# A two-block transformer step in fp32 on one core: negated maxima as a row of the queries, rotary halves added by transfers, input blocks and taps moved

## The reference

```python
u_l, cq_l, ckv_l, kr_l = mixer_inputs(x * (1 + sc1) + sh1, w_in[i])
k_nope_l, k_rope_l, v_l = mla_keys_values(ckv_l, kr_l, kv_norm_g[i], w_ukv[i], cos, sin)
q_nope_l, q_rope_l = mla_queries(cq_l, q_norm_g[i], w_uq[i], cos, sin)
attn_l = attend_blocked(...)          # softmax over 256 context and 512 own keys, 8 heads
conv_l = conformer_conv(u_l, conv_dw_w[i], conv_dw_b[i], conv_ln_g[i], conv_ln_b[i])
y_l = merge_groups(conv_l, attn_l, w_o[i], b_o[i])
x_mid = layer_norm(ALPHA * x + g1 * y_l, ln1_g[i], ln1_b[i])
f_l = conv_ffn(x_mid * (1 + sc2) + sh2, ...)

def attend(q_nope, q_rope, k_nope, k_rope, v):
    s = (q_nope . k_nope + q_rope . k_rope) * SOFTMAX_SCALE      # 64 and 32 wide
    return softmax(s) . v

def apply_rope(x, cos, sin):
    return jnp.concatenate([x1 * cos - x2 * sin, x2 * cos + x1 * sin], axis=-1)

def conformer_conv(u, dw_w, dw_b, ln_g, ln_b):       # u is 2 x 512 channels
    a, gte = jnp.split(u, 2, axis=-1)
    v = dwconv(a * jax.nn.sigmoid(gte), dw_w, dw_b)  # 31 taps, each channel for itself
    return jax.nn.silu(layer_norm(v, ln_g, ln_b))
```

## Time and profile before

| What | Value |
|---|---|
| median of 3 runs | 1101.9 us (1100.87 to 1102.03) |
| the profiled execution | 1101.06 us |
| its span, first to last instruction | 1099.2 us |
| TensorE busy | 98% |
| VectorE, ScalarE, GpSimd busy | 70%, 51%, 11% |
| mean granted clock of TensorE | 0.999 |
| weight stream and other HBM reads | 132.45 MB |

### The profile page before, as it was taken

How to read it: one execution, slowest core, us unless ns; L and a number is a source line. 1 busy time by engine, 2 the same in 40 slices (tenths; PEclk the granted TensorE clock), 3 DMA queues, 4 the chain that set the end, 5 groups by cost and what they waited for, 6 DMA issues and landing times.

```text
span 1099.2 us, 16381 instructions
## 1 busy us (share of the span) xinstructions
PE 1072.9 (98%) x6595; PEld 889.3 (81%) x6595; DVE 773.7 (70%) x1259; ACT 563.9 (51%) x1022; POOL 120.6 (11%) x152
## 2 busy tenths in 40 slices
PE   7989999999999999999999999999999999999997
PEld 4778888888888788888878777888888888888886
DVE  6978889878677747658886788777665656545427
ACT  6576566656333447764366775575444444431211
POOL 0222121112322000100211113000000000000001
PEclk9999999999999999999999999999999999999999
DMA  9743433346355753131342553222222323252202
GB/s 379 295 184 116 154 135 126 126 172 202 103 199 216 285 213 125 42 127 47 77 95 52 127 127 86 77 77 86 107 99 93 108 84 116 77 210 78 84 31 77
DMA packets 26550, 143.23 MB, mean 130 GB/s; under 512 B 3009, under 2 KB 3433, under 8 KB 12650
## 3 DMA queue, kind: packets, MB, share of 16 engines
q1 hardware_dynamic: 19936, 128.46, 32.6%
q0 software_dynamic: 4176, 7.60, 4.0%
q10 hardware_dynamic: 2362, 6.12, 1.6%
HBM read 132.45 MB, written 2.12 MB: 122 GB/s over the span
## 4 chain that ended last, share of the span: by engine, by line
PE 78%; DVE 10%; ACT 6%; issue 2%; DMA 2%; POOL 1%; DVEq 0%; SPq 0%; ACTq 0%; POOLq 0%
PE PB L185 76%; ACT WH L199 2%; DVE WL L206 2%; PE PB L193 2%; DVE RAW L1515 1%; DVE CV L214 1%; DMA RAW<-in_wstream 1%; POOL UPA L206 1%; DMA XL<-in_x 1%; DVE PX L237 1%; ACT XL L200 0%; DMA CV<-DG 0%; ACT L200 0%; ACT PTA L200 0%; DVE XL L214 0%
## 5 line engine op out<-in xcount | busy, mean ns | idle before, releaser
L185 PE MATMUL PB<-HH,WH 128*128 128x512 f32 (+1 forms) x880 | 338.4, 385 | 4.3 <-DVE HL L206 2.0
L185 PE MATMUL PB<-HH,WL 128*128 128x512 f32 (+1 forms) x880 | 333.0, 378 | 0.0
L206 DVE TENSOR_TENSOR WL<-RAW,WH 128x1024 fp32r<-128x1024 f32 (+3 forms) x172 | 196.5, 1149 | 192.3 <-ACT WH L199 191.9
L185 PE MATMUL PB<-HL,WH 128*128 128x512 f32 (+1 forms) x880 | 331.0, 378 | 0.0
L199 ACT ACTIVATE WH<-RAW 128x1024 fp32r<-128x1024 f32 (+3 forms) x172 | 166.8, 976 | 267.9 <-PE PB L185 231.7
L185 PEld LDWEIGHTS PB<-HH,WH 128*128 128x128 f32 x880 | 165.6, 188 | 36.8 <-issue 1.8
L185 PEld LDWEIGHTS PB<-HH,WL 128*128 128x128 f32 x880 | 165.6, 188 | 31.5 <-issue 0.2
L185 PEld LDWEIGHTS PB<-HL,WH 128*128 128x128 f32 x880 | 165.8, 188 | 29.7 <-issue 0.2
L185 PE MATMUL PB<-WL,AH 128*128 128x512 f32 (+1 forms) x198 | 72.5, 366 | 0.0
L185 PE MATMUL PB<-WH,AH 128*128 128x512 f32 (+1 forms) x198 | 72.5, 366 | 0.0
L185 PE MATMUL PB<-WH,AL 128*128 128x512 f32 (+1 forms) x198 | 72.4, 366 | 0.0
(11 more groups left out here) (308 smaller groups left out, 1748.2 us busy)
## 6 DMA issues: line engine op xcount, KB each, us to landing
RAW<-in_wstream SPq DMA_DIRECT2D x101, 1024.0 KB, 4.9
EARLY<-in_wstream SPq DMA_DIRECT2D x7, 1024.0 KB, 13.8
RAW<-in_wstream SPq DMA_DIRECT2D x5, 768.0 KB, 4.4
CV<-DG POOLq DMA_DIRECT2D x15, 256.0 KB, 3.3
TMP<-TMP POOLq DMA_DIRECT2D x14, 256.0 KB, 3.3
RAW<-in_wstream SPq DMA_DIRECT2D x5, 512.0 KB, 3.7
XL<-in_x SPq DMA_DIRECT2D x2, 1024.0 KB, 6.7
HB<-in_x SPq DMA_DIRECT2D x2, 1024.0 KB, 5.9
```

Source lines behind the costliest of these rows:

```text
L185: return self.put(lambda e: e.matmul(o, l, r, start=start, stop=stop, skip_group_check=skip))
L206: return self.put(lambda e: e.tensor_tensor(o, a, b, op))
```

## The change

1. **Maxima as a row.** `KR[96:128]` is no longer a copy: row 96 is one, the others zero. ScalarE copies only rows 0 to 95 of a query and writes into rows 96 to 127 the broadcast row of negated maxima, which TensorE makes once a head with the matrix of ones and `DGR` (`query_row`); the low part has zeros there (`no_rest`). A score tile then is three matmuls. In tile 0 of heads 0, 2, 4, 6 and 7 (`late`) the old form stays, over 96 rows, and the row is made behind it; for heads 1, 3 and 5 it is made between the two parts of the keys. There is one `DGR` instead of two.
2. **Rotary parts.** As the rows 96 to 127 no longer count, the two products are added explicitly: for heads 0 and 1 by VectorE (through `QS`), for the others by an accumulating transfer of 32 rows (`add_turned`), for which `query_high` waits; it moves from tile 4 to tile 5.
3. **Last input blocks.** `u2(3)` stands in the stream and on TensorE behind query 0, keys 0 and query 1, as blocks 88 and 89 instead of 84 and 85. The high parts of queries 0 and 1 overwrite two of its operand's tiles, hence the marks `("last", 0)` and `("last", 1)`.
4. **Taps.** The last six taps of tiles 0 and 2 are products on ScalarE and transfers (`more_product`, `add_more`) in tiles 1 and 5 of heads 0 to 5, so VectorE has 81 tap instructions. The square of tile 0 moves to tile 4 of head 3. The sums of the convolution tiles go from GpSimd to VectorE (`norm_sums`).

```diff
-QUERY_BLOCK, KEY_BLOCK, VALUE_BLOCK = (86, 89, 90, 92, 93, 96, 97, 99), (87, 91, 95, 98), (88, 94)
+QUERY_BLOCK, KEY_BLOCK, VALUE_BLOCK = (84, 86, 90, 92, 93, 96, 97, 99), (85, 91, 95, 98), (87, 94)
...
+    def late(h):
+        return h not in (1, 3, 5)
...
-    CONV_AT = {"75a": 2, "75b": 4, "76": 3, "78": 3, "79": 3, "81": 2, "82": 2, "83": 6, "84": 6, "85": 6, "86": 2, "86b": 2}
+    CONV_AT = {"75a": 2, "75b": 4, "76": 3, "78": 3, "79": 3, "81": 2, "82": 2, "83": 6, "84": 3, "85": 5, "85b": 3, "86": 2, "86b": 3}
...
+        def add_more(n):
+            j, k = more_of(n)
+            g.wait_ge(S_.a_cv, ("more", n))
+            g.wait_ge(S_.v_cv, ("tap", j, 24))
+            if n:
+                g.wait_ge(S_.added[2], ("more", n - 1))
+            g.put(lambda e: e.dma_start(CV[:, j, :], XBUF[n % 2], accum_op=ADD)).then_inc(S_.added[2], ("more", n), by=16)
+
+        def add_turned(h):
+            g.wait_ge(S_.v_ev, ("q", h))
+            g.put(lambda e: e.dma_start(TMPQ[64:96, :], TMPQ[96:128, :], accum_op=ADD)).then_inc(S_.turned, ("qr", h), by=16)
...
-            a.copy(QH[h % 3], TMPQ[:, :]).then_inc(S_.a_h, ("q", h))
+            a.copy(QH[h % 3][0:96, :], TMPQ[0:96, :]).then_inc(S_.a_h, ("q", h))
...
+        def query_row(h):
+            a.wait_ge(S_.p_sm, ("mr", h))
+            a.copy(QH[h % 3][96:128, :], aux.of(("mr", h))[96:128, :]).then_inc(S_.a_ax, ("mr", h))
...
                 power_of(h, t)
+                if t == 0 and late(h):
+                    query_row(h)
+                if t == 5 and h < 7 and not late(h + 1):
+                    query_row(h + 1)
+                if t == 5 and h < 6:
+                    query_high(h + 2)
...
+        def query_row(h):
+            bk = take_aux(("mr", h), 0)
+            pe.wait_ge(S_.a_s, "onesr")
+            pe.wait_ge(S_.a_s, ("dgr", h, 3))
+            pe.mm(bk, ONESR, DGR[:, :], True, True).then_inc(S_.p_sm, ("mr", h))
...
+            if direct:
+                pe.wait_ge(S_.a_s, "onesr")
+                pe.wait_ge(S_.a_s, ("dgr", h, 3))
+                op = pe.mm(bk, ONESR, DGR[:, :], False, True)
+            op.then_inc(S_.p_sm, ("s", h, t))
+            if direct:
+                query_row(h)
```

235 lines of the change are left out of this document (144 added, 91 removed).

## The result

The changed kernel takes **1113.9 us** (median of 4, 1112.1 to 1115.6), the one before 1102.0 us beside it: ratio **1.0108, interval [1.0092, 1.0124]**. It is 12 us slower, 13.9 us over the forecast and 8.9 us above the range's end. The profiled execution took 1113.75 us (span 1111.9 us).

What follows compares the result with a forecast made beforehand. The prediction took TensorE as the bound, busy for 1072.9 of 1099.2 us. Its terms +2.2 - 4.8 + 2.1 - 0.6 = -1.1 took the profiled 1101.06 us to 1100.0 us, with an 8 in 10 range of 1094.5 to 1105.

Steps and rivals of the forecast that it cites:

- Fewer matmuls: Attention loop: 48 matmuls with DGR become 13, each removed one worth 0.23 us, so 8.05 us saved at most.
- Entry: Entry of the loop: second maxima matmul of head 1 comes at 571.25 instead of 569.01 us, +2.2 us.
- Here VectorE decides: Entry of the loop: VectorE's added instructions and splits, less its earlier start, set the time; +2.2 us.
- shorter waits there are swallowed by this one: Entry: shorter TensorE waits while queries are prepared are absorbed by the wait for VectorE, so they add nothing.
- Inside a head: Within the loop's heads: removed matmuls are saved where TensorE is the bound; -4.8 us.
- From tile 1 to tile 3 TensorE is the bound: Inside a head: VectorE's extra 0.6 us fits into the 2.1 us of the next query's nine matmuls.
- Between two heads: Head changes in the loop: ScalarE, working in order with the row copy last, sets the time; +2.1 us.
- Transfers: GpSimd's added 256 KB and 64 KB transfers: landing 3.3 us after issue, late only over 4.9 us; 0 us.
- Rival 2: Loop: rotary halves land late, ScalarE stands at the query copy; 1105.5 us at 7 us landing; chance 0.17.
- After the loop: Convolution sums move from GpSimd to VectorE, so TensorE's idle 0.62 us before 681.78 goes; -0.6 us.
- Rival 3: GpSimd's issues are held while VectorE runs, each transfer starting up to 0.96 us later; 1101.2 us; chance 0.03.
- Rival 1: TensorE stays the bound between heads too, ScalarE being less behind; 1095.1 us, or 8.7 less with free entry; chance 0.30.

Runs made afterwards that it cites:

- v: b without VectorE's taps inside the loop except each group's first and last, these left out of the result; 1105.3 us, one run.
- b: The changed kernel with the twelve taps of tiles 0 and 2 back on VectorE, without their products and 256 KB transfers; 1108.2 us.
- d: The changed kernel with the last two input blocks ahead of the first queries again, orders at the entry adapted; 1121.3 us.
- f: b with blocks and entry order as before the change; 1111.6 us.
- w: b with two places in order changed: VectorE's rest of the queries later, two of ScalarE's exponentials ahead of diagonal blocks; 1109.4 us.
- u: b without the 23 tap products of group 1 in the loop and their 256 KB transfers, left out of the result; 1107.1 us, one run.
- a: The changed kernel with the rotary halves of heads 2 to 7 added by VectorE instead of by the 64 KB transfers; 1112.9 us.
- k: b with VectorE's rotary product split in two and the parts added by a GpSimd computing instruction instead of the 64 KB transfer; 1107.8 us.
- p: The kernel before the change with 13 unused spare matmuls in the wait at 67.5 us; 1101.2 us against 1102.5 us beside it.
- r: The changed kernel with unused spare matmuls in the waits at 67.5 us, at the entry and between heads 3 and 4; 1112.8 us.

## Why the prediction was wrong

- **Fewer matmuls, 8.05 us at most.** Right: 13 with DGR, 0.23 us apart at full clock.
- **Entry, +2.2.** Measured +4.1 (65.7 to 69.8 us). The first maxima of head 1 were read at 573.56, which less 1.8 us of a later start is 571.8, against 570.0 to 570.3. The step that failed is "Here VectorE decides": the wait of 2.17 us is for ScalarE's row copy, behind the zeros of a low part and three roundings, instructions of ScalarE for which the term has no price. VectorE has a part in it, as TensorE waited 1.06 and 0.40 us for its reductions ahead of that (564 us) and the diagonal's last part came 1.7 us late; how large is open, since v (entry 69.4 us, as in b) left out taps inside the loop alone. The other step that failed is "shorter waits there are swallowed by this one": they brought the clock down to 0.50, and the second maxima matmul came at 574.59. That the blocks' move itself costs was never tested by the prediction; d and f show that with the row in the queries it saves 2.8 us or more.
- **Inside a head, -4.8.** The step that failed most. "From tile 1 to tile 3 TensorE is the bound" had been true with four matmuls a tile; with three it reaches the queries and the next scores before single instructions that used to be in time, and ten waits of 7.6 us, some of them at the starts of heads, take nearly all of the 8.05; the loop before had 1.9 us of waits in all. VectorE's rest of the queries now stands ahead of the keys' rest; the prediction has no term for it, and it is 0.8 us three times, as w shows.
- **Between two heads, +2.1.** The mechanism was right, order and durations too (row copy 0.59, taken as 0.58). Between heads 3 and 4 the sum was 6.60 and 9.03 came, of which 2.15 is ScalarE's idle time for the transfer, which the sum had at nothing.
- **Transfers, 0.** The step that failed is "I take 0": the landing taken, 3.3 us, was that of the loop before, with 12 large transfers from GpSimd in place of 35. The 64 KB took 4.4 us in the median and 7.9 at the worst. Rival 2, at 0.17, named it: ScalarE idle ahead of HH<-TMPQ with a DMA as releaser. But it is not what made the kernel 12 us slower, as a has no such transfer and takes 1112.9 us. Its price at one transition is 1.8 to 2.3 us (b to k: 2.55 to 0.77; changed to a: 3.66 to 1.38), not 5.5 for three. By the Trainium skill (DMA: Bandwidth & Descriptors, Anatomy of one DMA) 64 KB take 2.15 us, an estimate; u's median of 2.4 is near it, and that sum has no term for other transfers in flight.
- **After the loop, -0.6.** Measured 6.85 to 6.08 us. With the sums on VectorE and the taps too it is 7.1, so the taps' move made it; but the kernel before shows 6.2 in p, so it is not firmly a gain.
- **Rival 3**: six issues of the small transfer took 0.79 to 1.49 us, 1.14 in the median; that of head 5, right behind another, 1.14. All four over 1.1 stand right behind another issue, and the two that do not took 0.79 and 0.80, so the queue of issues explains them and nothing of VectorE's hold is seen. Most of the large ones kept 0.87. **Rival 1** fell.
- **Not foreseen at all: the clock.** Some 1.7 us ahead of 504 us, 1.3 at the entry behind the row's wait (what it cost ahead of that wait ended in it), and 1.6 at 636 to 642 us. Taken out by spare matmuls it gave less: r has a median 1.1 us under the changed kernel's and an entry 0.6 us shorter. The Trainium skill (TensorE: Matmul & The Clock Gate, What's actually happening) has a gate that halves the clock by how busy TensorE has lately been; the rows above agree, with 0.50 behind waits.

The account of the loop, changed against before: +12.4 us of waits (14.3 against 1.9, from the queries of head 2 to the end), +1.6 of matmuls at half clock at 636 to 642 us and +0.4 at its start, -7.8 of 34 matmuls (the 35th is in the entry), is +6.6 of the 7.3 measured; 0.7 us stay open. Open too is how the entry's 3.4 us, which no run took back, divide between the row and the two rotary sums: the kernel before with the row and without any rotary sum was not tried.
